# A two-layer hybrid decoder trunk on one core: hardware loops over layers, heads and retention heads against a program written out in full

## What is computed

```
for l in range(DEPTH):                      # DEPTH = 2
    h = rmsnorm(x, norm_g); proj = h @ w_in            # 1024 x 9232
    o_r = retention(...)  for 4 heads (DK 128, DV 256, chunks of 128)
    o_d = gated_deltanet(...) for 8 heads (DK = DV = 128), q,k,v after a short causal conv
    y = sigmoid(gr) * (o_r @ w_up_r) + sigmoid(gd) * (o_d @ w_up_d)
    x = x + y @ w_o
return rmsnorm(x, final_gain)
```

## Time and profile before

| what | value |
|---|---|
| median of 3 runs | 2940.51 us |
| lowest, highest | 2935.75, 2943.71 us |
| the profiled execution's own time | 2926.58 us |
| its span, first to last instruction | 2924.8 us |
| mean granted TensorE clock | 0.987 |
| PE busy | 2796.9 us, 96% |
| PE weight loads (overlap PE) | 2311.8 us, 79% |
| DVE busy | 1725.4 us, 59% |
| ACT busy | 636.3 us, 22% |
| POOL busy | 882.1 us, 30% |

### The profile page before, as it was taken

One profiled execution on the slowest core, in us unless ns is written; L12 is line 12 of the kernel. 1 busy time (PEld: TensorE's weight loads), 2 busy tenths in 40 slices (PEclk: granted clock), 3 DMA queues, 4 the chain that ended last, 5 costly groups with the idle time before them and its releaser, 6 DMA issues.

```text
span 2924.8 us, 45951 instructions
## 1 busy us (share of the span) xinstructions
PE 2796.9 (96%) x14469; PEld 2311.8 (79%) x14469; DVE 1725.4 (59%) x3644; ACT 636.3 (22%) x1345; POOL 882.1 (30%) x473
## 2 busy tenths in 40 slices
PE   6999999999999999899979999999999999999997
PEld 4788888888878888788757888888888788877886
DVE  6687778777854334333567787678767434433346
ACT  5222222222211111200232222222222111111003
POOL 2323232323221212434432232323223111133443
PEclk8999999999999999999999999999999999999998
DMA  4312221223121111333522212221222111132245
GB/s 144 94 52 73 58 80 52 72 58 80 47 62 35 38 38 60 112 98 118 158 71 77 77 54 70 62 77 54 69 62 73 46 38 36 38 98 93 93 140 186
DMA packets 293245, 222.47 MB, mean 76 GB/s; under 512 B 32883, under 2 KB 248390, under 8 KB 292822
## 3 DMA queue, kind: packets, MB, share of 16 engines
q1 hardware_dynamic: 260534, 159.83, 19.8%
q10 hardware_dynamic: 32544, 60.83, 6.0%
HBM read 177.55 MB, written 43.06 MB: 75 GB/s over the span
## 4 chain that ended last, share of the span: by engine, by line
issue 72%; POOL 17%; PE 5%; DVE 2%; DMA 2%; ACT 1%; POOLq 1%; SPq 0%; DVEq 0%; ACTq 0%
POOL w_lo L1961 8%; POOL arena L2014 2%; POOL arena L2016 2%; POOL arena L2027 2%; PE dense_ps L711 1%; PE dense_ps L707 1%; PE dense_ps L709 1%; POOL arena L2031 1%; POOL act_lo L2073 1%; DMA w_raw<-in_w_out 1%; POOL arena L2021 1%; POOL act_lo L1974 0%; POOL arena L2055 0%; DMA arena<-row_scratch 0%; POOL act_lo L2048 0%
## 5 line engine op out<-in xcount | busy, mean ns | idle before, releaser
L707 PE MATMUL dense_ps<-act_hi,w_hi 128*128 128x512 f32 x2816 | 1179.0, 419 | 34.7 <-POOL act_lo L1974 11.5
L711 PE MATMUL dense_ps<-act_hi,w_lo 128*128 128x512 f32 x2816 | 1106.4, 393 | 0.0
L709 PE MATMUL dense_ps<-act_lo,w_hi 128*128 128x512 f32 x2816 | 1105.8, 393 | 0.0
L1961 POOL TENSOR_TENSOR w_lo<-w_raw,w_hi 128x1024 fp32r<-128x1024 f32 x192 | 494.7, 2577 | 1469.1 <-DVE w_hi L1408 1469.1
L707 PEld LDWEIGHTS dense_ps<-act_hi,w_hi 128*128 128x128 f32 x2816 | 533.2, 189 | 140.7 <-POOL act_lo L1974 13.3
L711 PEld LDWEIGHTS dense_ps<-act_hi,w_lo 128*128 128x128 f32 x2816 | 531.8, 189 | 117.5
L709 PEld LDWEIGHTS dense_ps<-act_lo,w_hi 128*128 128x128 f32 x2816 | 534.1, 190 | 87.8 <-issue 0.7
L1515 DVE SCALAR_TENSOR_TENSOR arena<-arena,cols 128x512 f32<-128x512 f32 x288 | 284.0, 986 | 12.6 <-DVE arena L1515 4.4
L1408 DVE CAST w_hi<-w_raw 128x1024 fp32r<-128x1024 f32 x192 | 132.5, 690 | 195.6 <-PE dense_ps L711 167.1
L690 PE MATMUL work<-mk,arena 128*128 128x128 f32 x896 | 132.7, 281 | 14.6 <-DMA arena<-in_x 5.9
L690 PEld LDWEIGHTS work<-mk,arena 128*128 128x128 f32 x896 | 110.2, 145 | 33.6 <-DVE arena L1836 7.3
(11 more groups left out here) (190 smaller groups left out, 3322.8 us busy)
## 6 DMA issues: line engine op xcount, KB each, us to landing
w_raw<-in_w_in SPq DMA_DIRECT2D x142, 512.0 KB, 3.6
arena<-l_scratch SPq DMA_DIRECT2D x32, 512.0 KB
gate_scratch<-arena ACTq DMA_DIRECT2D x64, 256.0 KB, 2.3
arena<-gate_scratch ACTq DMA_DIRECT2D x64, 256.0 KB, 3.0
w_raw<-in_w_out SPq DMA_DIRECT2D x18, 512.0 KB, 3.9
arena<-row_scratch SPq DMA_DIRECT2D x32, 256.0 KB, 4.3
o_scratch<-arena ACTq DMA_DIRECT2D x32, 256.0 KB, 2.0
arena<-o_scratch ACTq DMA_DIRECT2D x32, 256.0 KB, 3.3
```

The costliest lines, as they stand in the source:

```text
L707: eng.matmul(dense_ps[:, to, :], w_hi[:, slot, k, :], hi[:, k, seg], start=(k == 0), stop=False)
L709: eng.matmul(dense_ps[:, to, :], w_hi[:, slot, k, :], lo[:, k, seg], start=False, stop=False)
L711: mm = eng.matmul(dense_ps[:, to, :], w_lo[:, slot, k, :], hi[:, k, seg], start=False, stop=(k == KT - 1))
L1961: eng.tensor_tensor(w_lo[:, slot, :, :], w_from[second][:, :, :], w_hi[:, slot, :, :].bitcast(F32), ALU.subtract)\
```

## The change

On every engine the three hardware loops (`with eng.Fori(...)`) become Python loops, so each engine's list is written out in full, with no branch. `l`, `n`, `h` and `other` are then Python numbers, every `eng.snap(...)` is dropped, and every semaphore count and every DRAM address is a constant. The order of the steps on every engine, the buffers, the waits, their places and the DMAs stay the same. The core of the diff (the same edit recurs on all five engines):

```diff
-            with eng.Fori(0, DEPTH) as lay:
-                l = eng.snap(lay)
-                n = eng.snap(lay * NBLK)
-                other = eng.snap(lay * -1 + (DEPTH - 1))
+            for l in range(DEPTH):
+                n = l * NBLK
+                other = DEPTH - 1 - l
...
                 def l_blocks(u, half):
 
-                    t = eng.snap(l * (2 * DH) + u)
+                    t = (l * (2 * DH) + u)
...
-                with eng.Fori(0, DH - 2) as h:
+                for h in range(DH - 2):
                     unit_loads(h, True)
...
-                with eng.Fori(0, RH - 1) as h:
+                for h in range(RH - 1):
                     ret_loads(h, True)
...
-                    g = eng.snap(n + h * 6) if kind in ("even", "odd") else n
-                    tn = eng.snap(l * (2 * DH) + (2 * h + b + 1))
-                    t = eng.snap(l * (2 * DH) + (2 * h + b)) if kind != "first" else None
+                    g = (n + h * 6) if kind in ("even", "odd") else n
+                    tn = (l * (2 * DH) + (2 * h + b + 1))
+                    t = (l * (2 * DH) + (2 * h + b)) if kind != "first" else None
...
-                with eng.Fori(0, DH - 1) as h:
+                for h in range(DH - 1):
                     delta_unit("even", h)
                     delta_unit("odd", h)
```

More of the change, by code:

```diff
@@ L1167, in delta_unit @@
                           "odd_last": BLK_RET + 2}[kind]
[L1168 to L1173, removed]
+                    g = (n + h * 6) if kind in ("even", "odd") else n
+                    tn = (l * (2 * DH) + (2 * h + b + 1))
+                    t = (l * (2 * DH) + (2 * h + b)) if kind != "first" else None
+                    hn = (l * DH + (h + b))
+                    hz = (l * DH + h) if kind != "first" else None
+                    hc = (l * DH + (h + 1))
                     for step in unit_schedule(kind):
@@ L1628, in delta_unit @@
                         elif what == "gram":
-                            tw = eng.snap(tn + step[1])
+                            tw = (tn + step[1])
                             eng.wait_ge(gram_ps.sem, gram_ps.after(tw, 1))
@@ L1901, in _ @@
                         split_w(n + BLK_OUT + i + 2, i % 2, held=False,
-                                second=eng.snap(l * KT + (i + 2) // 2) if i % 2 == 0 else None)
+                                second=(l * KT + (i + 2) // 2) if i % 2 == 0 else None)
                     elif i == NHALF * KT - 2:
-                        split_w(n + NBLK + BLK_K0, 0, held=False, second=eng.snap(l * KT + KT))
+                        split_w(n + NBLK + BLK_K0, 0, held=False, second=(l * KT + KT))
                     else:
```

60 lines of the change are left out of this document (29 added, 31 removed).

## The result

The kernel after takes 2892.8 us (median of 4 runs, 2889.9 to 2896.82) beside 2941.45 us for the kernel before (4 runs, 2935.75 to 2943.71): ratio 0.9838, 95% interval 0.9820 to 0.9857, so 48.7 us or 1.6% less. The forecast was 12 us less, with a range that ended at 2914. The sign was right, the size wrong by four times. (One execution of a later run took 7610.7 us, over twice as long as any other; it is left out of that run's median.)

The account below looks back on a forecast made before the run. PE, busy 2796.9 of 2924.8 us, was taken to bound the kernel. Terms -4.4 - 4.3 - 1.0 - 1.4 - 2 + 1 gave -12 us, so 2928.5 us from 2940.5, range 2914 to 2940.

Parts of the forecast that it names:

- Step A: Change of layer: without DVE's branch back to the second layer its gap goes and PE waits less; gain 4.4 us.
- The rival in which the gap stays: Change of layer: DVE's gap is a fetch behind full DMA traffic and partly stays; 2933 us, chance 0.09.
- The other branches: nothing: DVE's loop over pairs: the 4.0 us behind its branch are covered by DVE's idle time, so no gain.
- step F: Pair and retention loops: about 54 more queue 8 packets, read as PE's instructions, may delay the solve's read; loss 1 us.
- Step B: Delta rule's late units: two register instructions of SP and one of DVE go, 0.27 us each of 16 units; gain 4.3 us.
- The bound of 29.3 us: Units: PE's waits for L1748, L1695 and L1736 together, taken as the most that step B could gain.
- The wider bound: Whole kernel: PE is idle 127.9 of 2924.8 us, at most which can be won.
- Steps C and D: Retention's register instructions on DVE, gain 1.0 us; weight blocks' ones between SP's wait and load, gain 1.4 us.
- E: First units, lifts and around the norms: some twenty PE waits with one exposed register instruction each; gain 2 us.
- The rival in which they stall PE: New block edges of PE in the loops: streamed instructions come late; +24 us, 2964 us, chance 0.09.
- The offset: Profiled execution lies 13.9 us below the median of the runs; carried over, 2914.6 us became 2928.5.
- The rival "more": Units: every exposed instruction on DVE's chain counts and B reaches 29.3 us; -37 us, 2903 us, chance 0.05.

Follow-up runs that it names:

- the run with registers: Kernel after, no branches, but DVE works out its semaphore counts in registers again: 2913.01 us, ratio 0.9899.
- the one with only the layer loop written out: Kernel before with the prefetch hint on DVE's pair loop, counts ahead of the first wait, and DVE's layer loop written out: 2919.77 us, ratio 0.9910.
- hint: Kernel before with a prefetch hint for the branch target at the top of DVE's loop over pairs: 2930.62 us, ratio 0.9952.
- the two other runs that have it and keep all loops: Kernel before with that prefetch hint, plus one on DVE's layer loop (2931.28 us), or plus DVE's counts ahead of the first wait (2929.59 us).
- the two traces of before: Unedited kernel before, profiled twice: span 2924.8 us in the forecast's execution, 2945.1 in the second, whose run measured 2943.9 us, ratio 1.0007.
- SP alone: Kernel before with only SP's list written out, all other engines keeping their loops: 2938.51 us, ratio 0.9968.
- SP on top of DVE: Kernel before with SP's and DVE's lists written out: 2896.15 us, ratio 0.9849; compared with only DVE's list written out: 2902.69 us, ratio 0.9858.
- The runs with additions: Kernel after with 3522 executed register additions on DVE, ahead of its waits (2912.08 us) or between waits and operation (3020.65 us).
- all but DVE written out: Kernel before with the lists of SP, PE, ACT and POOL written out, DVE keeping loops and registers: 2936.08 us, ratio 0.9968.

## Why the forecast was right or wrong

**Step A (change of layer, forecast 4.4 us): right.** PE's longest wait went from 8.26 to 3.88 us, 4.38 less, the mean starts 0.04 us behind L737, and ACT's table is there in time. DVE's gap goes with its branch, whatever else is kept (the run with registers, and the one with only the layer loop written out), and the 0.6 to 0.9 us of ACT's part go where ACT's loop is written out too. The rival in which the gap stays is out.

**"The other branches: nothing": this step failed.** Measured are 14 us (hint; the two other runs that have it and keep all loops give 12 and 16). The reasoning looked only at whether DVE was missed in those 4.0 us, and it wasn't. It did not ask what the fetch does to others: its packets stand among the unit's stores, whose landing SP awaits before the read. The prediction did weigh such a meeting, in step F, but only for the packets of queue 8 that were to come; the 29 of queue 14 that were there already, about five a pair, it passed over. The delay stands at the head of the chain stores, read, solve, state, on which PE then waits. From DVE's last operation ahead of the stores to the solve, a late unit took 13.14 and 13.71 us on average in the two traces of before, and 12.43 with the hint: 0.7 to 1.3 us, 14 times, is 10 to 18, and holds the 14. Of it, 0.5 to 0.7 us lie between the first store and the last landing, where the packets are; the other 0.2 to 0.6 lie in the read's flight, and why that is shorter is open.

**Step B (units, forecast 4.3 us): its term for DVE, one register instruction a late unit, was far too small; its instructions of SP were sized right.** For SP the forecast had two instructions of 0.09 us a late unit. In the traces, the way from DVE's last operation to the first store went from 0.24 to 0.17 us, from the stores' landing to the read's issue from 0.23 to 0.15, the issue itself from 0.63 to 0.60: 0.18 us together, 14 x 0.18 = 2.5 us (forecast 16 x 0.18 = 2.9). But SP alone measured 7 to 9 us, SP on top of DVE nothing to 10 (2902.7 and 0.9858 against 2896.2 and 0.9849, 2892.8 and 0.9838), so a few us of SP's are unexplained.

For DVE it had one instruction; its register instructions as a whole are worth 20 us by the times (2913.0 against 2892.8; 15 against the slowest of the three medians), 10 to 18 by the ratios. The runs with additions show that place decides most of such a cost. The term "those within the solve run while the operation before them does" nearly holds: the solve gained 9.57 - 9.35 = 0.2 us. Missed was the rest of the pair's chain: a pair is 96.4 us long with registers and 95.4 to 95.8 without. That is as much as six to ten exposed instructions of 0.095 us would cost, but they were not counted. What the traces place is a read that lands earlier, 6.13 to 6.35 us after the end of its issue instead of 6.64 with registers (and 6.81 and 7.22 in the two traces of before). The prediction took that flight as fixed but for PE's packets; what shortens it stays open.

**The bound of 29.3 us** was none. PE's three waits shrank by 24.0 us, but a pair of units went from 97.8 to 95.4 us, 14 x 2.4 = 33.6 us in all. Most of the difference was in PE's "busy" time: in 230 to 820 us it was 578.44 us for 3305 matmuls and is 589.17 for 3383, and at the old 0.1750 us a matmul those 3383 would have taken 3 us more, 7 over the 14 pairs. In a usual execution the waits alone were 38.8 us. The wider bound, the 127.9 us in which PE was idle, held: it is 92.6 us now.

**Steps C and D (1.0 and 1.4 us):** waits 1.3 and 1.4 us smaller, as forecast, though no run takes either alone. **E** was not measured by itself.

**Step F (streamed instructions of PE, a loss of 1):** 62 more packets on queue 8, forecast 54, of 1.1 us each by their own records, forecast 0.9. Their price is not visible: all but DVE written out takes as long as SP alone. The rival in which they stall PE is refuted; no wait of PE by "issue" is new (four at one line before and after, 4.7 and 4.4 us in all). That queue 8 is PE's stays a reading: it moves the 62 packets only where PE's, ACT's and POOL's lists are all written out.

**The offset.** The profiled execution lay 13.9 us below the median, and that was carried over. About half of what set that execution apart, 9.5 us of 20, lay in the very waits that the change removes, and the kernel after has its profiled execution at 2889.9, only 2.9 below its median of 2892.8. For the profiled execution itself the forecast was 2914.6 us and the measured time 2889.9, so of the 35.7 us by which the median was missed, the offset is 11; the other 24.7 are the terms above.

**The sum** now: branch over pairs 14, change of layer 4, register work of DVE 10 to 20, SP 3 to 9: 31 to 47 of 48.7 us, with C and D inside (its interval is 42 to 53). The rival "more" (2903, chance 0.05) was nearest; but its place would be luck: its condition, that every exposed instruction on DVE's chain counts, may hold for the 10 to 20 us of DVE's registers, and it has no term for the branch over pairs.

**On the page "Runtime: NRT & Kernel Launch" of the Trainium skill**, section "Instruction fetch mechanics": that a taken branch outside the held window makes its engine fetch before it goes on agrees with the gaps of 4.0 and 5.59 us, which both vanish with the branch. The same section calls the step from one block of a list to the next mostly hidden; this agrees with the lists written out here, where no wait of PE by "issue" is new. Of a taken branch it tells the stall of the engine itself; in the loop over pairs that stall was hidden on DVE, and the time was lost at SP's stores. The 128 KB store for TensorE in the section "ISA Cache" of the Trainium skill's page "Advanced Engine Details and Errata" agrees with queue 8, if it is PE's, resting within the loops before and moving 62 packets more after. In this kernel these cost nothing that the runs can see.

## What to carry to other kernels

Where an engine's branch is hidden behind idle time of its own, look at what its instruction fetch runs into: here the last of eight small stores, which SP awaits, landed 0.4 to 0.5 us later on average, on a chain for which PE waits. A register instruction costs little ahead of a wait (about 3 ns on average here) and 0.09 us between a wait and its operation; on a chain of thirty short steps that decides. And take the count of the bounding engine's instructions in a window, not its busy share, as the measure of what can be won, from more than one execution.

## What was not expected of the hardware

- Two packets of instructions of 8 KB, fetched behind DVE's branch among a unit's eight stores, go with a landing of the last store after 1.83 to 1.91 us on average instead of 1.45.
- 62 more packets of 16 KB on queue 8, beside steady loads of 68 GB/s, cost nothing measurable.
- A hint at the top of the loop over pairs brings the next instruction from 4.0 to 0.4 us behind the branch, and no packet of DVE's instructions moves in that loop any more; at the loop over layers the hint does nothing (5.72 us of idle time).
- 3583 register instructions ahead of their waits still cost some 11 us (5 to 20 by the different measures), about 3 ns each, on an engine that is 40% idle.
